# Two-layer hybrid decoder: fewer, larger groups of small matmuls between the dense ones, another order on VectorE between the mLSTM heads, and half chunks scored as couples of 64 rows

## The reference

```
for i in range(DEPTH):                       # two layers
    h = rmsnorm(x, norm1[i])
    if i % 2 == 0: mix, xq = mlstm_mixer(h, ...)      # conv + silu on q, k; gates; 4 heads of 192
    else:          mix, xq = diff_attention(h, ...)   # q, k norms, rotary, softmax pairs, 6 heads
    xo = memory_cross_attention(xq, mem, ...)         # q, k norms, softmax over 256 memory tokens
    x = x + concat([mix, xo]) @ w_out[i]
    h = rmsnorm(x, norm2[i])
    gu = h @ w_gate_up[i]
    x = x + (silu(gu[..., :FFN]) * gu[..., FFN:]) @ w_down[i]
```

## Time and profile before

| | |
|---|---|
| median of three runs | 1249.49 us |
| the profiled execution | 1249.32 us |
| its span, first to last instruction | 1247.5 us |
| PE matmul busy in the span | 1234.5 us (99%) |
| POOL / DVE / ACT busy | 843.2 / 519.3 / 346.6 us |
| PE busy, layer A's heads (143 to 246 us) | 101.0 of 103 us |
| PE busy, layer B's heads (670 to 862 us) | 190.9 of 192 us |
| granted TensorE clock, mean of the span | 1.000 |

### The profile page before, as it was taken

The page is one execution under the profiler, slowest core; times in us unless marked ns, Lnnn a source line. Parts: engine busy times, 40 slices in busy tenths (PEclk is TensorE's granted clock), DMA queues, the critical chain, the costliest instruction groups (busy, mean ns, idle before and its releaser), DMA issues.

```text
span 1247.5 us, 15936 instructions
## 1 busy us (share of the span) xinstructions
PE 1234.5 (99%) x5786; PEld 997.1 (80%) x5786; DVE 519.3 (42%) x798; ACT 346.6 (28%) x687; POOL 843.2 (68%) x1032
## 2 busy tenths in 40 slices
PE   7999999999999999999999999999999999999998
PEld 6888877788888888888888777778888888888887
DVE  6954434743332232213344877775432112221321
ACT  6522444633220011101141566645322001100110
POOL 7898333566877777777776344445777777776775
PEclk9999999999999999999999999999999999999999
DMA  7234211132232222222233222222222223223223
GB/s 258 102 118 151 70 51 35 52 102 81 96 101 99 87 101 101 96 89 101 76 131 98 85 69 68 62 76 66 85 95 90 102 101 101 86 99 101 89 75 105
DMA packets 35066, 116.98 MB, mean 94 GB/s; under 512 B 4417, under 2 KB 4930, under 8 KB 34886
## 3 DMA queue, kind: packets, MB, share of 16 engines
q1 hardware_dynamic: 33272, 112.22, 26.7%
q10 hardware_dynamic: 1742, 4.10, 1.2%
HBM read 111.05 MB, written 2.11 MB: 91 GB/s over the span
## 4 chain that ended last, share of the span: by engine, by line
PE 94%; DVE 3%; POOL 1%; ACT 1%; issue 1%; ACTq 0%; DMA 0%; SPq 0%; DVEq 0%; POOLq 0%
PE PS L1505 92%; PE PS L1896 1%; POOL w_lo L554 1%; DVE nmB L1411 0%; DVE tmp L1261 0%; ACTq L858 0%; PE PS L1742 0%; DMA w_raw<-in_wt_dram 0%; DVE Al L1237 0%; PE PS L1924 0%; DVE WT L1189 0%; ACT PB L893 0%; DVE PS L1409 0%; PE PS L1851 0%; PE PS L1859 0%
## 5 line engine op out<-in xcount | busy, mean ns | idle before, releaser
L554 POOL TENSOR_TENSOR w_lo<-w_raw,w_hi 128x256 fp32r<-128x256 f32 x804 | 619.1, 801 | 17.1
L549 POOL TENSOR_SCALAR w_hi<-w_raw 128x1024 fp32r<-128x1024 f32 (+2 forms) x205 | 213.0, 1039 | 373.3 <-PE PS L1505 372.7
L1505 PE MATMUL PS<-Hh,w_hi 128*128 128x512 f32 x1072 | 432.1, 403 | 6.8 <-POOL w_lo L530 6.6
L1505 PE MATMUL PS<-Hh,w_lo 128*128 128x512 f32 x1072 | 418.8, 391 | 0.0
L1505 PE MATMUL PS<-Hl,w_hi 128*128 128x512 f32 x1072 | 418.5, 390 | 0.0
L1505 PEld LDWEIGHTS PS<-Hh,w_hi 128*128 128x128 f32 x1072 | 201.8, 188 | 61.1 <-issue 22.0
L1505 PEld LDWEIGHTS PS<-Hh,w_lo 128*128 128x128 f32 x1072 | 201.7, 188 | 43.1
L1505 PEld LDWEIGHTS PS<-Hl,w_hi 128*128 128x128 f32 x1072 | 202.1, 189 | 37.9 <-issue 1.0
L1505 PE MATMUL PS<-Ah,w_hi 128*128 128x512 f32 (+1 forms) x544 | 208.1, 382 | 0.1
L1505 PE MATMUL PS<-Ah,w_lo 128*128 128x512 f32 (+1 forms) x544 | 205.0, 377 | 0.0
L1505 PE MATMUL PS<-Al,w_hi 128*128 128x512 f32 (+1 forms) x544 | 204.9, 377 | 0.0
(11 more groups left out here) (248 smaller groups left out, 965.1 us busy)
## 6 DMA issues: line engine op xcount, KB each, us to landing
w_raw<-in_wt_dram SPq DMA_DIRECT2D x181, 512.0 KB, 3.3
w_raw<-in_wt_dram SPq DMA_DIRECT2D x16, 384.0 KB, 3.1
w_raw<-in_wt_dram SPq DMA_DIRECT2D x8, 448.0 KB, 3.2
QKR<-QKP ACTq DMA_DIRECT2D x24, 128.0 KB, 4.3
xT<-in_x_t_dram SPq DMA_DIRECT2D x8, 256.0 KB, 5.9
out_dram<-xT SPq DMA_DIRECT2D x8, 256.0 KB, 2.0
mT<-in_mem_t_dram SPq DMA_DIRECT2D x1, 1024.0 KB, 9.5
cn<-in_constants_dram ACTq DMA_DIRECT2D x1, 580.5 KB, 5.9
```

The source lines that it names most:

```text
L549: nc.gpsimd.tensor_scalar(w_hi[:, sl, 0:nk], w_raw[:, raw, 0:nk], 0.0, 1.0, ALU.add, ALU.mult).then_inc(w_round, 1)
L554: lo = nc.gpsimd.tensor_tensor(w_lo[:, sl, w], w_raw[:, raw, w], w_hi[:, sl, w].bitcast(F32), ALU.subtract)
L1505: return nc.tensor.matmul(out_, a, b, start=start, stop=stop)
```

## The change

- `head_scores` issues all four full-chunk matmuls first, then the four half-chunk ones. These use 64 rows only: the blocks 0 and 2 the rows where the head's half lies, the blocks 1 and 3 the other 64 rows, where SP has put copies of that half of q and k (QSW, KSW) by eight DMAs. Nothing is zeroed any more, so two memsets on DVE go, and ACT's silu of two chunks is one instruction instead of two.
- `head_turn` runs whole behind block 7 of the second tile.
- On DVE `head_diag(h + 1)` and `m_p(h)` stand directly behind `m_max(h)`, ahead of `head_out(h)`.
- In layer B sums of squares of two blocks go into one group, likewise the four transposes of `b_kbc` and of `b_oturn`; `b_vt` moves one block earlier; `c_pv` moves to block 2 of the third tile, directly ahead of `b_s(c, 3)`. Layer A's `cross_ss` goes in two groups instead of four.

```diff
+                if n in (T_HEAD + 1, T_HEAD + 5):
+                    i = (n - T_HEAD) // 4
+                    c = HALF_CHUNK[i]
+                    sp.wait_ge(qk_ready, MC + c + 1)
+                    for r in (0, 64):
+                        sp.dma_start(QSW[64 - r:P - r, i], QK[r:r + 64, c]).then_inc(sw_in[i], 16)
+                        sp.dma_start(KSW[64 - r:P - r, i], QK[r:r + 64, MC + c]).then_inc(sw_in[i], 16)
...
+            head_diag(0)
             for h in range(MH):
-                head_diag(h)
                 head_p(h)
-                if h >= 1:
-                    m_p(h - 1)
...
                 m_max(h)
+                if h < MH - 1:
+                    head_diag(h + 1)
+                m_p(h)
                 if h == MH - 1:
-                    m_p(h)
                     fill_out(2 * h + 1)
                 head_out(h)
...
                     mm(o, QK[:, MC + f, s * P:(s + 1) * P], QK[:, f, s * P:SEQ], stop=False)
-                    kz = KZ[:, HALF_CHUNK.index(c)] if r else QK[:, MC + c]
-                    mm(o, kz[:, s * P:(s + 1) * P], QK[:, c, s * P:SEQ], start=False).then_inc(s_done, 1)
+                pe.wait_ge(sw_in[i], 64)
+                for s in range(NT):
+                    o = PS[:, S_BANK[s], s * P:SEQ]
+                    if s % 2:
+                        w, m, q = KSW[64 - r:P - r, i], QSW[64 - r:P - r, i], s
+                    else:
+                        w, m, q = QK[r:r + 64, MC + c], QK[r:r + 64, c], s
+                    mm(o, w[:, q * P:(q + 1) * P], m[:, q * P:SEQ], start=False).then_inc(s_done, 1)
...
-                    if k >= KD - 2:
-                        head_turn(h, k - (KD - 2))
+                    if k == KD - 1:
+                        head_turn(h)
...
+                    if k < 2:
+                        for t in (2 * k, 2 * k + 1):
+                            b_ss(c, 0, t)
+                            b_ss(c, 1, t)
...
+                    if x is not None and k == 2:
+                        c_pv(x)
                     if k in (0, 2):
                         b_s(c, 2 + k // 2)
-                    if x is not None and k == 3:
-                        c_pv(x)
```

More of the change, by code:

```diff
@@ L215, in hybrid_trunk @@
         V = sb("V", [P, NT, MH * VW], scope=sA)
-        KZ = sb("KZ", [P, 2, SEQ], scope=sA)
+        QSW = sb("QSW", [P, 2, SEQ], scope=sA)
+        KSW = Ah[:, 0:2].bitcast(F32)
         Mrow = sb("Mrow", [MH, SEQ], scope=sA)
@@ L321, in hybrid_trunk @@
         v_ones = sem("v_ones")
-        k_zero = sem("k_zero")
+        sw_in = [sem(f"sw_in{i}") for i in range(2)]
         m_rows = nc.dram_tensor("m_rows", (MH, SEQ), F32).ap()
@@ L462, in hybrid_trunk @@
         MIXED = [QK[:, c] for c in range(MC)]
-        MIXED[1], MIXED[4] = QK[:, MC], KZ[:, 0]
+        MIXED[1], MIXED[4] = QK[:, MC], QSW[:, 0]
         block = ctx.enter_context(nc.Block())
@@ L639, in silu @@
                 y = PS[:, CV_BANK[c % 2]]
[L640 to L645, removed]
+                nc.scalar.activation(QK[:, c], y, ACT.Silu).then_inc(qk_ready, 1)
             def v_out(c):
@@ L1098, in _ @@
             nc.vector.tensor_reduce(rm[:], msq, AX.X, ALU.add).then_inc(msum_done, 1)
-            dve.wait_ge(msum_done, 1)
-            nc.vector.memset(KZ[0:64], 0.0)
-            nc.vector.memset(QK[64:P, MC + 1:MC + 5:3], 0.0).then_inc(k_zero, 1)
             v_raw(0)
@@ L1658, in head_scores @@
                     pe.wait_ge(kn_ready, 2)
+                i = HALF_CHUNK.index(c)
                 for s in range(NT):
@@ L1687, in head_pv, with head_turn @@
                         last.then_inc(num_done, 1)
-            def head_turn(h, p):
+            def head_turn(h):
                 f, (c, r) = FULL[h], HALF[h]
[L1692 to L1699, removed]
-                full, half = f * P - h * MHD, c * P + r - h * MHD
[L1701 to L1706, removed]
+                full, half = f * P - h * MHD, c * P + r - h * MHD
+                pe.wait_ge(hn_low, 2 * h + 2)
+                pe.wait_ge(p_ready, NT * (h + 1))
+                if h == 1:
+                    pe.wait_ge(v_ready, V_DONE[-1])
+                pe.wait_ge(hn_high, 2 * h + 2)
+                for t in range(NT):
+                    at = (t % 2) * MHD + full
+                    nc.tensor.transpose(PS[:, 6, t * P:(t + 1) * P], t512[3 + t // 2][:, at:at + P], ident)
+                for t in range(NT):
+                    at = (t % 2) * MHD + half
+                    last = mm(PS[r:r + 64, 7, t * P:(t + 1) * P], t512[3 + t // 2][:, at:at + 64], ident)
+                last.then_inc(ht_done, 1)
             def cross_ss(l, c, t):
@@ L1755, in in_first @@
                 def in_first(k):
-                    if h == 0 and 3 <= k < 3 + NT:
-                        cross_ss(0, 0, k - 3)
-                        cross_ss(0, 1, k - 3)
+                    if h == 0 and k in (3, 5):
+                        for t in (k - 3, k - 2):
+                            cross_ss(0, 0, t)
+                            cross_ss(0, 1, t)
                     if h == 1 and k == 1:
@@ L1976, in in_q @@
                         b_t(c - 1, 2 + k)
-                    if c >= 1 and k == 2:
+                    if k < 2:
+                        for t in (2 * k, 2 * k + 1):
+                            b_ss(c, 0, t)
+                            b_ss(c, 1, t)
+                    if c >= 1 and k == 1:
                         b_vt(c - 1)
-                    if k < NT:
-                        b_ss(c, 0, k)
-                        b_ss(c, 1, k)
                     if c >= 1 and k == 4:
@@ L1990, in in_k @@
                 def in_k(k):
[L1992 to L1997, removed]
+                    if k == 0:
+                        for t in range(NT):
+                            b_kbc(c, t)
+                    if c >= 1 and k == 2:
+                        for t in range(NT):
+                            b_oturn(c - 1, t)
                     if k == 4:
```

## The result

The changed kernel takes 1251.07 us (median of 22 runs, 1248.39 to 1255.24) against 1249.45 us of before (22 runs, 1249.12 to 1250.07): ratio 1.0014, 95% interval 1.0008 to 1.0021. It is 0.14% slower, where I forecast 1248.9 us, a little faster. The spread is the first thing to see: the 22 runs of before lie within 1 us, those after within 7 us, and in steps that follow the mean granted clock of TensorE. Seven runs at 1.000 have a mean of 1248.6 us, four at 0.999 lie about 1250.2, four at 0.997 about 1252.3, six at 0.996 about 1253.5, and one at 0.995 at 1255.24. The clock is on record for 75 further runs of before, and all are at 1.000.

A forecast was written before the change was run, and what follows sets the result against it. TensorE, holding 94% of the chain of waits, bounds the kernel. Terms -0.2 - 1.4 - 1.7 - 1.7 - 0.3 + 6.3 - 1.6 = -0.6 us give 1248.7, with the median's 0.17 us 1248.9 us; range 1243.8 to 1252.0 us.

The forecast's parts named there:

- the new wait: Scores of heads 1 to 3: block 2 waits 2.1 us each for head_out, behind m_p on DVE; +6.3 us.
- slower: Outcome that the whole kernel gets slower: chance 0.12, of which 0.11 from the couples.
- the couples: Half chunks of layer A's scores: 64-row matmuls run together in pairs, 0.43 us saved per head; -1.7 us.
- Plain groups: Some 25 fewer groups of small matmuls, each costing 0.02 us at most beyond its passes; -0.2 us.
- c_pv with b_s: Layer B: c_pv directly ahead of b_s(c, 3) shares its group and covers a wait, 0.39 us per chunk; -1.6 us.
- One turn: Whole turn behind block 7: the fixed 0.34 us is paid once instead of twice per head; -1.4 us.
- they do not run together: Rival, half chunks of all four heads: each pair's matmuls run one after the other; +5.0 us, 1253.9 us, chance 0.12.
- m_t's waits: Cross unit's transposes in heads 0 to 2 no longer wait for m_p, which runs earlier; -1.7 us.
- Behind head 3: m_t's wait there shrinks because POOL starts its split earlier and m_p meets less of it; -0.3 us.
- free of POOL: Rival: m_p in the heads never meets POOL's split, +0.3 instead of +6.3 us; 1242.9 us, chance 0.10.
- held once: Rival: only one running POOL instruction holds m_p, +2.4 instead of +6.3 us; 1245.0 us, chance 0.10.
- Layer B gave nothing back: Answers a rival: earlier c_pv only moves PE to its next wait, losing the -1.6 us; 1250.5 us, chance 0.08.

The follow-up runs named there:

- mp_on_act: The changed kernel with m_p's four scalings taken by ScalarE instead of VectorE, behind the next head's weights: 1242.29 us, ratio 0.9942.
- wait_longer: The changed kernel with 256 columns of head_out's first scaling done once more ahead of it in heads 0 to 2: 1254.85 us, ratio 1.0041.
- layer_b_alone: The kernel before with only layer B's part of the change (fewer, merged groups, c_pv ahead of b_s(c, 3)): 1247.84 us, ratio 0.9989.
- order_alone: The kernel before with only VectorE's new order (next head's mask and m_p ahead of head_out): 1247.53 us, ratio 0.9986.
- before_idle_2: The kernel before with hout awaited at block 0 and 256 columns of head_out's first scaling done twice in heads 0 to 2: 1257.37 us, ratio 1.0058.

## Why the prediction was wrong

The step that failed is **the new wait**, +6.3 us for three. Its story and its length were right: m_p beside the split, ahead of head_out, block 2 third; 1.94 to 2.07 us each by the listed waits, 0.16 us more by starts, 6.4 us in all. The full-clock runs lie 1248.6 - 1242.3 = 6.3 us over mp_on_act, which keeps some 0.5 us of these waits and frees 0.4 us of m_t behind head 3. But I priced the wait at its own length only. Behind it PE ran at half clock about every second time, 34 falls in 22 runs, and that adds 2.6 us on average, more than all that the sum had left. The sum without it, -0.6 us, compares with 1248.6 - 1249.45 = -0.8 us. I had asked for each wait what is queued behind it, and not at what clock that queue would run. None of the rivals had this price either: "slower" got its 0.12 nearly all for the couples, which ran together as forecast. The range of 1246.3 to 1250.8 us that I gave the forecast itself is worked out from none of its terms, and 0.2% was too much for what a measurement can tell from no change: with 22 runs each, 0.14% is clear of its interval.

The trace of before has no wait as long as this inside the heads, where its longest is 0.9 us, so it could not say what 2 us would do. It has one row that could have raised the question, at the program's start:

```profile
6.55 0.77 PE L1505 MATMUL PS<-Hh,w_hi 128*128 128x512 f32 x1 [6.55 <-POOL w_lo L530]
...
11.95 0.63 PE L1505 MATMUL PS<-Hh,wg 128*128 128x512 f32 x1
12.38 0.56 PE L1505 MATMUL PS<-Hl,w_hi 128*128 128x512 f32 x1
12.77 0.39 PE L1505 MATMUL PS<-Hl,wg 128*128 128x512 f32 x1
13.01 0.40 PE L1505 MATMUL PS<-Hh,w_hi 128*128 128x512 f32 x1
```

Behind a wait of 6.55 us the dense matmuls start 0.43 us apart up to 12.38, the stride that they also have in the recorded half-clock stretch of wait_longer (204.16 to 204.59), and 0.23 us apart afterwards. The mean of 1.000 in the table of before does not show it, because the clock's record begins only at 12.7 us.

The other terms, by what the runs showed:

- Plain groups (-0.2) and c_pv with b_s (-1.6): layer_b_alone gained 1.6 us, of which 4 x 0.357 = 1.4 are the joint groups, by starts, and some 0.1 the plain groups. The joint group came out at 0.357 us less, not 0.39: the switch inside it costs 0.19 us, where I took 0.15. The Trainium skill (TensorEngine Tiling (Array Packing), Key Properties) says that a change of the tiling mode drains TensorE. The estimate of -1.4 that I had worked out by that agrees with the measured 1.43.
- One turn (-1.4): 0.35 us per head, right. Its side effect on POOL, 1 us earlier, was in the sum too.
- Couples (-1.7): 0.475 us in head 0, so 4 x 0.475 = -1.9 but for what block 2 waits in heads 1 to 3; right in kind. That they do not run together is out.
- m_t's waits (-1.7): order_alone gained 1.9 us; right. Behind head 3 (-0.3): m_t's group costs 0.50 us less.
- The rivals on m_p: free of POOL is out (3.08 us beside it), and so is held once. Layer B gave nothing back.

Each of these is within 0.3 us of its forecast, so the full-clock time is no luck. They also add up without the wait: in mp_on_act the groups cost, by starts, 1.4 us less at the couples, 1.4 at the turns, 1.9 at m_t of heads 0 to 2, 0.9 at m_t of head 3 and 1.5 in layer B, 7.1 us of the 7.2 measured.

## What to carry to other kernels

In this kernel a wait of TensorE inside dense work had two prices: its length, and the half-clock stretch that may follow. Where a change makes a wait of about 2 us, look for the granted clock behind it, and expect runs that differ in steps. A gain that moves one engine's start can put two others side by side: before an instruction is put in front of one that TensorE waits for, see what GpSimd will be doing by then, and whether ScalarE has room for it instead.

## What the hardware showed that I had not expected

An idle time of about 2 us in the midst of dense work was enough for the granted clock to go down to 0.50, 1.2 GHz, for 3.4 us: 34 falls for 66 waits in the changed kernel, 8 for 15 in before_idle_2. DVE's scalings and POOL's instructions took turns: between heads 1 and 2 the four scalings of m_p end 0.14 to 0.15 us behind the ends of POOL's first four instructions, one by one. Beside the split each scaling took about 0.81 us, against 0.35 alone (medians of the 16 in each trace), and a start 0.63 us ahead of POOL instead of 0.38 behind it was worth 1.15 us of the four (3.08 against 1.93). And two 64-row matmuls of unequal length ran together: 512 and 384 columns start 0.01 us apart, and the scores of head 0 take 3.85 us, where the row of equal ones gives 2.12 + 1.69 = 3.81.
